# Latent rows, keys and values of the last token tile, made in the softmax attention's first group

## Chip, cores and metric

One core of a Trainium2 chip (trn2). The metric is the device time of one execution in microseconds (us); a kernel's time is the median of its runs.

## What is computed

One inference step of a decoder layer over a prompt of 1024 tokens (8 tiles of 128) and 8 single sample tokens. One input projection feeds two head groups: latent attention with softmax (8 heads) and gated linear attention, called GLA (4 heads). Their gated outputs go through one output projection and a layer norm. Cut to what matters here:

```python
q = (rms_norm(cq, q_norm_g) @ w_uq)             # queries, 8 heads of 64 + 32 (rotary)
ckv = rms_norm(ckv, kv_norm_g)                  # latent rows, 128 wide
kr = apply_rope(kr, cos, sin)                   # one rotary key for all heads
k_nope = einsum('bsr,rhn->bshn', ckv, w_uk)     # keys of the prompt
v      = einsum('bsr,rhv->bshv', ckv, w_uv)     # values of the prompt
# query block i (128 tokens) attends to keys of tiles 0..i
p = softmax(where(key_pos <= q_pos, s * MLA_SCALE, -inf)); o = p @ v
# GLA: chunkwise, with a state carried from tile to tile
state = exp(b_last) * state + (k * exp(b_last - b)).T @ v
```

## The kernel before

Every engine's instructions are written out by hand, in order, and engines meet through counting semaphores (`x.wait_ge(sem, n)` waits until a count is reached). T is 8, the number of token tiles. PSUM is addressed as `banks[:, 0..7, 512]`.

After the input projection come eight **slots**, `for k in range(T)`, one for each token tile of the GLA. On TensorE slot k runs, in this order: `latent_rows(k+1)` (L2014, four transposes of the next tile's latent query part, latent rows and rotary key into bank 6), `decays(k+1, 0)`, `forget_gate`, `near_products(k)` in three parts (L2090, 32 x 32 products) with `decays(k+1, 1)` between, `latent_keys(k+1)` (L2023, four products with `w_uk` into bank 6), the third part of `near_products(k)`, `far_products(k)`, the rest of the decays, `key_query_rows(k+2)`, `latent_values(k+1)` (L2029, one product with `w_uv` into bank 2), `gated_columns(k-1)` and `outputs(k)` (L2118, L2121, and L2126 for the state). `near_products(k)` waits for `S_ready` of tile k-1: VectorE (DVE) makes the new state at L1561 from the products of L2126. Slot 6 also holds the two `q_proj` of query block 0's tile (L2152), slot 7 their transposes (L2161) and the first scores (`head_scores(0)`, L2174).

The products of 32-bit operands run as two passes each, so one `nc.tensor.matmul` of them appears as two MATMUL records, each with a weight load (LDWEIGHTS, engine PEld).

ScalarE (ACT) brings the results out of PSUM: `latent_out` (L1068: L1073, L1074, L1075), `latent_keys_out` (L1077: L1080, twice) and `latent_values_out` (L1083: L1086). After each tile's rotary key is in place, SyncE (SP) spreads it to all heads by a DMA (L779).

Then come the 48 **steps** of the softmax attention, in four groups of 12. `GROUPS = ((6, 0), (4, 3), (5, 2), (7, 1))` names the query blocks of each group, and `TURNS[0] = "LLLLSLLSLLSS"` the order in the first group: L is one head of block 6, S two heads of block 0. Query block i reads keys and values of tiles 0 to i, so the last tile's keys and values are first read by block 7, in the fourth group (from step 36). Step s on TensorE: `head_scores(s)`; HEAD place; then at the TAIL place `weights_turned(s-2)` (L2383), `products(p)` of a finished pair of heads (L2302, before the table's pieces); then what the tables put there: `q_proj` and `q_transpose` of later query blocks through bank 7. ACT in step s: HEAD place; `transposed_out(s-2)` (L1253), `probabilities(s)` (L1244), TAIL place, where `q_half` (L1142) and `qt_half` (L1148) empty bank 7. DVE in step s: `mix` of a pair, the largest scores (L1710 and L1712), and the normalising of the step before (L1728).

Of the kernel before, what the change touches and what calls it, by code (L numbers as in the profile page):

```python
# [15 lines left out]
P = 128  # L16
# [88 lines left out]
def hybrid_step(nc, a, o):  # L105

    with ExitStack() as ctx:
# [483 lines left out]
        def q_bank(i, q):  # L591

            return 6 if i == 0 and q == 0 else 7

        def mixed_bank(t):

            return 1 if t < T - 2 else 6
# [19 lines left out]
                     (32, HEAD), (32, TAIL), (35, TAIL), (36, TAIL), (37, TAIL), (39, TAIL), (40, TAIL), (42, TAIL), (44, TAIL)]  # L617
        assert len(PIECES_AT) == PIECES and sorted(PIECES_AT) == PIECES_AT
        assert not set(PIECES_AT) & (set(PROJECTED_AT) | set(TURNED_AT))

        def piece_at(s, place):
            return PIECES_AT.index((s, place)) + 1 if (s, place) in PIECES_AT else 0
# [100 lines left out]
        def _(sp):  # L723
# [111 lines left out]
        def _(pool):  # L835
# [111 lines left out]
        def _(act):  # L947
# [120 lines left out]
            def latent_out(t):  # L1068
                act.wait_ge(a_transposed, t + 1)
                if t > 0:  # L1070
                    act.wait_ge(k_done, t)
                    act.wait_ge(kv_done, t)
                nc.scalar.activation(ckvT, banks[:, 6, QR:QR + P], ACT.Copy).then_inc(a_copied, 1)  # L1073
                nc.scalar.activation(z[:, t, 0:QR], banks[:, 6, 0:QR], ACT.Copy).then_inc(a_copied, 1)  # L1074
                nc.scalar.activation(KTh[NOPE:QK, 0, P * t:P * t + P], banks[NOPE:QK, 6, 384:512], ACT.Copy).then_inc(a_copied, 1)  # L1075

            def latent_keys_out(t):  # L1077
                act.wait_ge(k_done, t + 1)
                for q in range(2):
                    nc.scalar.activation(KTh[0:NOPE, q:H:2, P * t:P * t + P],  # L1080
                                         banks[NOPE * q:NOPE * q + NOPE, 6, :].rearrange("p (h s) -> p h s", h=4), ACT.Copy).then_inc(k_copied, 1)

            def latent_values_out(t):  # L1083
                act.wait_ge(kv_done, t + 1)
                act.wait_ge(kdec_ready, t + 1)
                nc.scalar.activation(z[:, t, W_GQ:W_GV], banks[:, 2, :], ACT.Copy).then_inc(v_copied, 1)  # L1086

            def key_query_out(t):
                act.wait_ge(qk_transposed, t + 1)
# [81 lines left out]
            for k in range(T):  # L1171
                if k == T - 1:
                    for q in range(2):
                        qt_half(0, q)
                if 0 <= k + 1 < T:
                    latent_out(k + 1)
                    decay(k + 1, 0)
                if k + 2 < T:
                    n_a = soft(k + 2)
                if 0 <= k + 1 < T:  # L1180
                    decay(k + 1, 1)
                    latent_keys_out(k + 1)
                if k >= 0:
                    far_blocks(k)
                if 0 <= k + 1 < T:
                    decay(k + 1, 2)
                    decay(k + 1, 3)
                    decay_rest(k + 1)
                if k + 2 < T:
                    key_query_out(k + 2)  # L1190
                if k == T - 2:
                    for q in range(2):
                        q_half(0, q)
                if 0 <= k + 1 < T:
                    latent_values_out(k + 1)
                if 0 <= k < T - 1:
                    n_a = o_stats(k)
# [88 lines left out]
            for s in range(len(STEPS) + LAG):  # L1286
                if s == 2:
                    act.wait_ge(gated_T, T)
                    act.wait_ge(S_out, 32)
                for place in (HEAD, TAIL):  # L1290
                    if place == TAIL:
                        if s == len(STEPS):
                            act.wait_ge(qt_done, 2 * T)
                        if s >= len(STEPS):
                            for j in range(2):
                                keys_out(0, 2 * (s - len(STEPS)) + j)
                        if s >= LAG:
# [590 lines left out]
        def _(pe):  # L1888
# [124 lines left out]

            def latent_rows(t):  # L2014
                pe.wait_ge(normed, 1)
                pe.wait_ge(qkT_copied, 2 * max(t, 1) + 2)
                if t == 1:
                    pe.wait_ge(k_copied, 2)
                for q in range(3):
                    nc.tensor.transpose(banks[:, 6, P * q:P * q + P], z[:, t, P * q:P * q + P], ident[:])  # L2020
                nc.tensor.transpose(banks[0:QK, 6, 384:512], z[:, t, W_KR - NOPE:W_GM], ident[:]).then_inc(a_transposed, 1)

            def latent_keys(t):  # L2023
                pe.wait_ge(a_copied, 3 * t + 3)
                for m in range(H // 2):
                    last = nc.tensor.matmul(banks[:, 6, P * m:P * m + P], w_uk[:, P * m:P * m + P], ckvT, start=True, stop=True)
                last.then_inc(k_done, 1)

            def latent_values(t):  # L2029
                if t > 0:  # L2030
                    pe.wait_ge(att_copied, 6 * t)
                nc.tensor.matmul(banks[:, 2, :], ckvT, w_uv[:], start=True, stop=True).then_inc(kv_done, 1)

            def gate_rows(t):
                if t > 0:
# [40 lines left out]
            def near_products(t, levels):  # L2076
                if levels[0] == 0:
                    pe.wait_ge(x_ready, t + 1)
                    pe.wait_ge(v_copied, t + 1)
# [169 lines left out]
            pe.wait_ge(padded, 6)  # L2249

            for k in range(T):
                if 0 <= k + 1 < T:
                    latent_rows(k + 1)
                    decays(k + 1, 0)
                if k + 2 < T:
                    forget_gate(k + 2)
# [6 lines left out]
                if 0 <= k + 1 < T:  # L2263
                    latent_keys(k + 1)
                if k == T - 1:
                    for q in range(2):
# [9 lines left out]
                    key_query_rows(k + 2)  # L2276
                if k == T - 2:
                    q_proj(0, 0)
                if 0 <= k + 1 < T:
                    latent_values(k + 1)  # L2280
                if k + 3 < T:
                    gate_rows(k + 3)
# [130 lines left out]
            for s in range(len(STEPS) + LAG):  # L2413
# [6 lines left out]
                for place in (HEAD, TAIL):  # L2420
                    if place == TAIL:
# [6 lines left out]
                        if s >= LAG:  # L2428
# [4 lines left out]
                            for p in range(N_PAIRS_OF_HEADS - 2):  # L2433
                                if last_step(p) == r - 1:
                                    products(p)
                    if (s, place) in PROJECTED_AT:
                        bank_of_queries((s, place))
                        q_proj(*PROJECTED_AT[s, place])
# [201 lines left out]
```

## Time and profile before

| | us |
|---|---|
| median of 3 runs | 745.68 |
| the runs | 745.23, 745.68, 751.47 |
| the profiled execution, its own time | 743.97 |
| span from its first to its last instruction | 742.1 |
| TensorE busy | 705.5 (95% of the span) |
| VectorE busy | 355.3 (48%) |
| ScalarE busy | 327.3 (44%) |
| GpSimd busy | 75.6 (10%) |

The mean granted TensorE clock is 0.995 of full speed. Slot 6 stands at 353.3 to 366.9 us of the span, slot 7 from there to 375.7, and steps 4 to 6 of the softmax attention at 388.7 to 399.7. The ends of matmuls are modelled, so two records that follow each other overlap in the listing; what a stretch of TensorE costs is read from the start of its first instruction to the start of the one behind it.

### The profile page before, as it was taken

The numbers are of one execution on the slowest core, as the hardware profiler recorded it, in microseconds if no ns is written. First come the engines' busy times: TensorE is split into PE (matmuls) and PEld (weight loads), VectorE is DVE, ScalarE is ACT, GpSimd is POOL, SyncE is SP. The second block draws the span as 40 slices with busy tenths as digits, with TensorE's granted clock in tenths as the row PEclk, the third lists the DMA queues.
The fourth block names the chain that finished last, engine by engine and source line by source line (L and its number), as shares of the span: only waits on it lengthen the run. The fifth ranks groups of instructions, "written<-read, shape, count | busy, mean of one in ns | idle before, by whom it ended". The sixth has DMA issues, their size and how long they took to land.

```text
span 742.1 us, 16684 instructions
## 1 busy us (share of the span) xinstructions
PE 705.5 (95%) x7025; PEld 546.4 (74%) x7025; DVE 355.3 (48%) x782; ACT 327.3 (44%) x779; POOL 75.6 (10%) x113
## 2 busy tenths in 40 slices
PE   2799999999999999999999999999999999999995
PEld 1486878788789986777766666777677889678884
DVE  0454380030202025777675576667671111389977
ACT  1254651121212137667656566645675667602100
POOL 0000000000000010101111201132113443000000
PEclk9999999999999999999999999999999999999999
DMA  9995300303001011000010000202756774103332
GB/s 293 396 375 174 114 0 1 114 0 97 0 1 57 1 43 51 9 14 11 10 11 1 1 1 1 59 1 76 240 183 222 274 267 175 60 1 116 123 132 85
DMA packets 35301, 70.31 MB, mean 95 GB/s; under 512 B 6626, under 2 KB 17979, under 8 KB 33564
## 3 DMA queue, kind: packets, MB, share of 16 engines
q1 hardware_dynamic: 30602, 47.73, 19.8%
q0 software_dynamic: 4016, 20.97, 8.1%
q8 instruction: 56, 0.92, 0.5%
q10 hardware_dynamic: 610, 0.55, 0.3%
q14 instruction: 17, 0.14, 0.1%
HBM read 62.26 MB, written 6.07 MB: 92 GB/s over the span
## 4 chain that ended last, share of the span: by engine, by line
PE 90%; DVE 3%; SPq 2%; DMA 2%; ACT 1%; issue 1%; another core or an unknown queue 1%; DVEq 0%; ACTq 0%
PE banks L1988 21%; PE banks L2174 8%; PE banks L2000 6%; PE banks L2302 5%; PE banks L2383 4%; PE banks L2403 3%; PE banks L2152 3%; PE banks L2512 3%; PE banks L2514 3%; PE banks L2513 2%; PE banks L2090 2%; PE banks L2009 2%; PE banks L2452 2%; PE banks L2471 2%; PE banks L2495 2%; DMA s_x<-in_x_prompt 2%
## 5 line engine op out<-in xcount | busy, mean ns | idle before, releaser
L1044 ACT ACTIVATE s_z<-banks 128x512 f32<-128x512 f32 (+3 forms) x40 | 19.6, 501 | 130.0 <-PE banks L1988 130.0
L1988 PE MATMUL banks<-s_w_parts,s_h_b 128*128 128x272 f32 (+3 forms) x328 | 68.0, 323 | 0.0
L1253 ACT ACTIVATE s_z<-banks 128x512 f32<-128x512 f32 (+2 forms) x88 | 41.4, 517 | 47.1 <-PE banks L2383 46.3
L1417 DVE COPY s_zs<-banks 8x512 f32<-8x512 f32 (+3 forms) x6 | 3.5, 576 | 118.5 <-PE banks L1962 118.5
L1988 PEld LDWEIGHTS banks<-s_w_parts,s_h_b 128*128 128x128 f32 x328 | 49.3, 189 | 4.9 <-issue 1.7
L1244 ACT ACTIVATE s_z<-banks,s_temps 128x896 f32<-128x896 f32 (+7 forms) x64 | 47.2, 742 | 11.6 <-DVE s_temps L1712 8.6
L1988 PE MATMUL banks<-s_w_parts,s_h_a 128*128 128x256 f32 (+2 forms) x256 | 49.7, 314 | 0.0
L1988 PE MATMUL banks<-s_z_r,s_h_b 128*128 128x512 f32 (+1 forms) x152 | 48.8, 387 | 0.0
L2383 PEld LDWEIGHTS banks<-s_ident,s_z 128*128 128x128 f32 x288 | 33.3, 141 | 11.8 <-issue 5.5
L2383 PE MATMUL banks<-s_ident,s_z 128*128 128x128 f32 x288 | 39.8, 274 | 1.6 <-DVE s_z L1728 1.6
L1988 PE MATMUL banks<-s_z_r,s_h_a 128*128 128x512 f32 x128 | 40.9, 395 | 0.0
L1988 PEld LDWEIGHTS banks<-s_w_parts,s_h_a 128*128 128x128 f32 x256 | 36.0, 189 | 3.6 <-issue 0.4
L2302 PE MATMUL banks<-s_z 128*64 128x128 f32 x576 | 38.5, 278 | 0.0
L1267 ACT ACTIVATE s_z<-banks 128x512 f32<-128x512 f32 x64 | 33.1, 602 | 9.3 <-PE banks L2403 7.6
L2302 PEld LDWEIGHTS banks<-s_z 128*64 128x64 f32 x576 | 30.8, 136 | 5.4 <-issue 5.4
L1350 ACT ACTIVATE s_temps<-s_temps,s_eps_t 128x1 f32<-128x1 f32 (+1 forms) x9 | 2.6, 294 | 72.2 <-DVE s_temps L1845 72.2
L1728 DVE TENSOR_SCALAR s_z<-s_z,s_temps 128x896 f32<-128x896 f32 (+7 forms) x64 | 33.2, 540 | 1.7
L1712 DVE TENSOR_REDUCE s_temps<-banks 128x1 f32<-128x896 f32 (+3 forms) x32 | 32.8, 1024 | 1.1
L1988 PEld LDWEIGHTS banks<-s_z_r,s_h_b 128*128 128x128 f32 x152 | 28.5, 188 | 5.6
L1988 PEld LDWEIGHTS banks<-s_z_r,s_h_a 128*128 128x128 f32 x128 | 24.0, 188 | 6.7 <-issue 0.8
L2174 PE MATMUL banks<-s_kt,s_temps 96*128 96x512 f32 (+1 forms) x64 | 25.9, 527 | 0.0
L2174 PE MATMUL banks<-s_kt,s_z 96*128 96x512 f32 (+2 forms) x64 | 25.2, 515 | 0.0
(391 smaller groups left out, 1520.7 us busy)
## 6 DMA issues: line engine op xcount, KB each, us to landing
s_z<-in_w_ada SPq DMA_DIRECT2D x16, 512.0 KB, 12.2
s_temps<-in_w_in SPq DMA_DIRECT2D x3, 2048.0 KB, 7.7
s_x<-in_x_prompt SPq DMA_DIRECT2D x8, 512.0 KB, 11.8
s_z<-in_w_ada SPq DMA_DIRECT2D x1, 4096.0 KB, 13.8
s_kt<-in_w_out SPq DMA_DIRECT2D x8, 512.0 KB
s_temps<-in_x_prompt SPq DMA_DIRECT2D x8, 512.0 KB
out_y_prompt<-s_temps SPq DMA_DIRECT2D x7, 512.0 KB
s_temps<-in_w_in SPq DMA_DIRECT2D x2, 832.0 KB, 14.2
```

The source lines that it names most:

```text
L1244: last = nc.scalar.activation(weights_of(s, u), score_of(s, u), ACT.Exp, bias=nmx[:, c:c + 1], accum_out=rsum[:, c:c + 1])
L1253: nc.scalar.activation(PTb[r % 3][:, 4 * g:4 * g + n, :], banks[:, 4 + (groups(r) + g) % 2, 0:P * n].rearrange("p (j q) -> p j q", j=n), A ...
L1267: nc.scalar.activation(latT(n, j), banks[:, j, :], ACT.Copy).then_inc(f_Tc, 1)
L1712: nc.vector.tensor_reduce(nmx[:, c:c + 1], score_of(s, 0), AX_X, ALU.max, negate=True).then_inc(mx_ready, 1)
L1728: last = nc.vector.tensor_scalar(weights_of(s, u), weights_of(s, u), rinv[:, c + u:c + u + 1], None, ALU.mult)
L1988: last = nc.tensor.matmul(banks[:, proj_bank(c, t), 0:WIDTH[c]], h_[half][:, k, n0:n0 + P], w_, start=(k == 0 and n == 0), stop=(k == KT - ...
L2000: last = nc.tensor.matmul(banks[:, proj_bank(1, u), :], w_[:, k, P * m:P * m + P], h_[half][:, k, :], start=(k == 0 and n == 0), stop=(k = ...
L2152: last = nc.tensor.matmul(banks[:, q_bank(n, q), 0:384], z[:, BLOCKS[n], P * k:P * k + P], w_uq[:, k, 384 * q:384 * q + 384], start=(k == ...
L2174: last = nc.tensor.matmul(score_of(s, u)[:, n0:n1], QTb[n % 4][:, h, :], KTh[:, h, n0:n1], start=True, stop=True)
L2302: last = nc.tensor.matmul(banks[64 * par:64 * par + 64, 6, 0:P], V(j, 2 * hp + par), block, start=(j == 0), stop=(j == i))
L2383: last = nc.tensor.transpose(banks[:, 4 + k0 % 2, P * (b % 4):P * (b % 4) + P], Pm[r % 3][:, P * b:P * b + P], ident[:])
L2403: last = nc.tensor.transpose(banks[:, j, P * r:P * r + P], cached(n, 4 * j + r), ident[:])
```

## The change

The three pieces of the last token tile (t = 7) leave slot 6 and go to three places of steps 4 and 5: the rows to (4, HEAD), the keys to (5, HEAD), the values to (5, TAIL), on TensorE and ScalarE alike. They use bank 7 in place of banks 6 and 2. The latent rows, transposed, go to the tile's own slab `z[:, 7, W_CKV:W_KR]` and not to `ckvT`, so ScalarE first waits for the output DMA that reads that slab (`kv_out`). The spreading DMA of the last tile moves behind SP's later transfers, GpSimd's wait becomes one tile shorter, and the scores of block 7 get the waits that were in slots 6 and 7.

```diff
+        def latent_bank(t):
+            return 6 if t < T - 1 else 7
+        def turned_latent(t):
+            return ckvT if t < T - 1 else z[:, T - 1, W_CKV:W_KR]
+        LAST_ROWS_AT, LAST_KEYS_AT, LAST_VALUES_AT = (4, HEAD), (5, HEAD), (5, TAIL)
...
 # SP
-            for t in range(T):
+            for t in range(T - 1):
+                rotary_keys_spread(t)
...
             sp.dma_start(o_new[:, :, 0:KVR], o["kv_sample"][:, :, 0, :].to_broadcast([H, NB, KVR])).then_inc(p_rows, 16)
+            rotary_keys_spread(T - 1)
...
 # POOL
-            pool.wait_ge(a_copied, 3 * T)
+            pool.wait_ge(a_copied, 3 * (T - 1))
...
 # ACT, latent_out(t)
+                if t == T - 1:
+                    act.wait_ge(kv_out, 32)
...
 # ACT, the slots
-                if 0 <= k + 1 < T:
-                    latent_out(k + 1)
+                if k + 1 < T - 1:
+                    latent_out(k + 1)
...
 # ACT, the steps
+                    if (s, place) == LAST_ROWS_AT:
+                        latent_out(T - 1)
+                    if (s, place) == LAST_KEYS_AT:
+                        latent_keys_out(T - 1)
+                    if (s, place) == LAST_VALUES_AT:
+                        latent_values_out(T - 1)
...
 # PE, latent_rows(t), latent_keys(t), latent_values(t)
+                if t == T - 1:
+                    pe.wait_ge(qp_copied, projected_before(LAST_ROWS_AT))
...
+                if t == T - 1:
+                    pe.wait_ge(qp_copied, projected_before(LAST_KEYS_AT))
...
+                if t == T - 1:
+                    pe.wait_ge(k_copied, 2 * T)
...
 # PE, q_proj(0, 0)
-                    pe.wait_ge(k_copied, 2 * T)
+                    pe.wait_ge(k_copied, 2 * (T - 1))
...
 # PE, head_scores(s)
+                if i == T - 1:
+                    pe.wait_ge(kr_in, 16 * T)
+                    pe.wait_ge(k_copied, 2 * T)
...
 # PE, slot 7
-                    pe.wait_ge(kr_in, 16 * T)
+                    pe.wait_ge(kr_in, 16 * (T - 1))
...
 # PE, bank_of_queries(at): before each q_proj and q_transpose of the steps
+                if at > LAST_ROWS_AT:
+                    pe.wait_ge(a_copied, 3 * T)
+                if at > LAST_VALUES_AT:
+                    pe.wait_ge(v_copied, T)
```

## Rows read from the trace of the kernel before

**Rows 1.** Stretch of steps 4, 5: span, busy time (count) of each engine, PEclk, DMA.
```profile
389.09:396.80 7.71, 7.71 (x56) 5.24 (x55) 3.61 (x10) 4.01 (x11) 2.33 (x4) 1.00 0.01 3
```
**Rows 2.** TensorE in order of time, slots 6, 7: start, us, instruction, idle before.
```profile
353.29 0.55 PE L2020 MATMUL banks<-s_ident,s_z 128*128 128x128 f32 x3
...
353.70 0.48 PE L2066 MATMUL banks<-s_act_parts,s_w_parts 128*128 128x512 f32 x1
...
354.34 0.35 PE L2090 MATMUL banks<-s_mixT 64*32 64x32 f32 x32
...
357.57 0.49 PE L2026 MATMUL banks<-s_temps,s_w_uk 128*128 128x128 f32 x3 [0.37 <-issue]
...
357.99 0.76 PE L2090 MATMUL banks<-s_temps 64*32 64x32 f32 x64
...
361.87 1.02 PE L2032 MATMUL banks<-s_w_uv,s_temps 128*128 128x512 f32 x2
362.73 0.60 PE L2139 MATMUL banks<-s_ident,s_temps 128*128 128x128 f32 x4
...
367.74 0.36 PE L2090 MATMUL banks<-s_mixT 64*32 64x32 f32 x32 [0.80 <-DVE s_temps L1561]
...
368.95 1.08 PE L2161 MATMUL banks<-s_ident,s_z 128*96 128x128 f32 x8
```
**Rows 3.** VectorE in order of time: the state of tiles 5, 6.
```profile
353.41 0.60 DVE L1561 SCALAR_TENSOR_TENSOR s_temps<-s_temps,banks 128x128 f32<-128x128 f32 x2 [0.19 <-PE banks L2126]
...
366.99 0.61 DVE L1561 SCALAR_TENSOR_TENSOR s_temps<-s_temps,banks 128x128 f32<-128x128 f32 x2 [2.33 <-PE banks L2126]
```
**Rows 4.** TensorE again: keys of slot 6 up to their pause, and of slot 5.
```profile
356.38 0.82 PE L2026 MATMUL banks<-s_temps,s_w_uk 128*128 128x128 f32 x5
...
345.15 1.16 PE L2026 MATMUL banks<-s_temps,s_w_uk 128*128 128x128 f32 x8
346.24 0.29 PE L2090 MATMUL banks<-s_temps 64*32 64x32 f32 x16
346.69 0.61 PE L2090 MATMUL banks<-s_temps 64*32 64x32 f32 x48 [0.16 <-issue]
```
**Rows 5.** The same view in slot 2, a longer pause.
```profile
311.66 0.25 PE L2107 MATMUL banks<-s_temps 64*32 64x32 f32 x4 [1.03 <-issue]
```
**Rows 6.** Counts between pauses (PE, then PEld, in brackets), and behind the last.
```profile
311.64:346.69 35.05, 34.77 (x757) 25.82 (x758) 26.59 (x80) 24.94 (x83) 2.25 (x4) 1.00 0.06 13
346.69:357.56 10.87, 10.51 (x253) 8.18 (x253) 8.04 (x25) 7.91 (x27) 1.41 (x3) 1.00 0.01 4
357.56:366.07 8.51, 8.50 (x126) 6.07 (x126) 5.67 (x17) 4.94 (x11) 0.84 (x2) 1.00 0.07 17
```
**Rows 7.** DMA queues at 309.3 to 309.4, 355.2 to 355.3 and 363.3 to 363.4.
```profile
q8 instruction: 1, 0.02, 57.6%
...
q8 instruction: 1, 0.02, 57.5%
...
q8 instruction: 1, 0.02, 60.0%
```
**Rows 8.** ScalarE in order of time, slot 6 and steps 3 to 5.
```profile
358.10 1.21 ACT L1080 ACTIVATE s_kt<-banks 64x512 f32<-64x512 f32 x2 [0.74 <-PE banks L2026]
...
388.87 0.50 ACT L1142 ACTIVATE s_z<-banks 128x384 f32<-128x384 f32 x1
...
395.23 0.98 ACT L1253 ACTIVATE s_z<-banks 128x512 f32<-128x512 f32 x2 [1.51 <-PE banks L2383]
...
396.19 1.01 ACT L1244 ACTIVATE s_z<-banks,s_temps 128x896 f32<-128x896 f32 x1
```
**Rows 9.** TensorE in order of time, steps 4 to 6.
```profile
389.09 0.93 PE L2383 MATMUL banks<-s_ident,s_z 128*128 128x128 f32 x7
...
394.53 0.93 PE L2383 MATMUL banks<-s_ident,s_z 128*128 128x128 f32 x7
395.30 1.67 PE L2174 MATMUL banks<-s_kt,s_z 96*128 96x512 f32 x4
```

More of the change, by code:

```diff
@@ L619, in hybrid_step @@
         assert not set(PIECES_AT) & (set(PROJECTED_AT) | set(TURNED_AT))
+        LAST_ROWS_AT, LAST_KEYS_AT, LAST_VALUES_AT = (4, HEAD), (5, HEAD), (5, TAIL)
+        assert not {LAST_ROWS_AT, LAST_KEYS_AT, LAST_VALUES_AT} & (set(PROJECTED_AT) | set(TURNED_AT) | set(PIECES_AT))
         def piece_at(s, place):
@@ L776, in _, with rotary_keys_spread @@
             sp.dma_start(w_uq[:], a["w_uq"].rearrange("(k p) n -> p k n", p=P)).then_inc(uq_in, 16)
-            for t in range(T):
+            def rotary_keys_spread(t):
                 sp.wait_ge(a_copied, 3 * t + 3)
@@ L1072, in latent_out @@
                     act.wait_ge(kv_done, t)
-                nc.scalar.activation(ckvT, banks[:, 6, QR:QR + P], ACT.Copy).then_inc(a_copied, 1)
-                nc.scalar.activation(z[:, t, 0:QR], banks[:, 6, 0:QR], ACT.Copy).then_inc(a_copied, 1)
-                nc.scalar.activation(KTh[NOPE:QK, 0, P * t:P * t + P], banks[NOPE:QK, 6, 384:512], ACT.Copy).then_inc(a_copied, 1)
+                if t == T - 1:
+                    act.wait_ge(kv_out, 32)
+                nc.scalar.activation(turned_latent(t), banks[:, latent_bank(t), QR:QR + P], ACT.Copy).then_inc(a_copied, 1)
+                nc.scalar.activation(z[:, t, 0:QR], banks[:, latent_bank(t), 0:QR], ACT.Copy).then_inc(a_copied, 1)
+                nc.scalar.activation(KTh[NOPE:QK, 0, P * t:P * t + P], banks[NOPE:QK, latent_bank(t), 384:512], ACT.Copy).then_inc(a_copied, 1)
             def latent_keys_out(t):
@@ L1080, in latent_keys_out @@
                     nc.scalar.activation(KTh[0:NOPE, q:H:2, P * t:P * t + P],
-                                         banks[NOPE * q:NOPE * q + NOPE, 6, :].rearrange("p (h s) -> p h s", h=4), ACT.Copy).then_inc(k_copied, 1)
+                                         banks[NOPE * q:NOPE * q + NOPE, latent_bank(t), :].rearrange("p (h s) -> p h s", h=4), ACT.Copy).then_inc(k_copied, 1)
             def latent_values_out(t):
@@ L1085, in latent_values_out @@
                 act.wait_ge(kdec_ready, t + 1)
-                nc.scalar.activation(z[:, t, W_GQ:W_GV], banks[:, 2, :], ACT.Copy).then_inc(v_copied, 1)
+                nc.scalar.activation(z[:, t, W_GQ:W_GV], banks[:, 2 if t < T - 1 else 7, :], ACT.Copy).then_inc(v_copied, 1)
             def key_query_out(t):
@@ L1181, in _ @@
                     decay(k + 1, 1)
+                if k + 1 < T - 1:
                     latent_keys_out(k + 1)
@@ L1193, in _ @@
                         q_half(0, q)
-                if 0 <= k + 1 < T:
+                if k + 1 < T - 1:
                     latent_values_out(k + 1)
@@ L2015, in latent_rows @@
                 pe.wait_ge(normed, 1)
-                pe.wait_ge(qkT_copied, 2 * max(t, 1) + 2)
+                pe.wait_ge(qkT_copied, min(2 * T, 2 * max(t, 1) + 2))
                 if t == 1:
                     pe.wait_ge(k_copied, 2)
+                if t == T - 1:
+                    pe.wait_ge(qp_copied, projected_before(LAST_ROWS_AT))
                 for q in range(3):
-                    nc.tensor.transpose(banks[:, 6, P * q:P * q + P], z[:, t, P * q:P * q + P], ident[:])
-                nc.tensor.transpose(banks[0:QK, 6, 384:512], z[:, t, W_KR - NOPE:W_GM], ident[:]).then_inc(a_transposed, 1)
+                    nc.tensor.transpose(banks[:, latent_bank(t), P * q:P * q + P], z[:, t, P * q:P * q + P], ident[:])
+                nc.tensor.transpose(banks[0:QK, latent_bank(t), 384:512], z[:, t, W_KR - NOPE:W_GM], ident[:]).then_inc(a_transposed, 1)
             def latent_keys(t):
                 pe.wait_ge(a_copied, 3 * t + 3)
+                if t == T - 1:
+                    pe.wait_ge(qp_copied, projected_before(LAST_KEYS_AT))
                 for m in range(H // 2):
-                    last = nc.tensor.matmul(banks[:, 6, P * m:P * m + P], w_uk[:, P * m:P * m + P], ckvT, start=True, stop=True)
+                    last = nc.tensor.matmul(banks[:, latent_bank(t), P * m:P * m + P], w_uk[:, P * m:P * m + P], turned_latent(t), start=True, stop=True)
                 last.then_inc(k_done, 1)
             def latent_values(t):
-                if t > 0:
+                if t == T - 1:
+                    pe.wait_ge(k_copied, 2 * T)
+                elif t > 0:
                     pe.wait_ge(att_copied, 6 * t)
-                nc.tensor.matmul(banks[:, 2, :], ckvT, w_uv[:], start=True, stop=True).then_inc(kv_done, 1)
+                nc.tensor.matmul(banks[:, 2 if t < T - 1 else 7, :], turned_latent(t), w_uv[:], start=True, stop=True).then_inc(kv_done, 1)
             def gate_rows(t):
@@ L2078, in near_products @@
                     pe.wait_ge(x_ready, t + 1)
-                    pe.wait_ge(v_copied, t + 1)
+                    pe.wait_ge(v_copied, min(t + 1, T - 1))
                     if t > 0:
@@ L2251, in _ @@
             for k in range(T):
+                if k + 1 < T - 1:
+                    latent_rows(k + 1)
                 if 0 <= k + 1 < T:
-                    latent_rows(k + 1)
                     decays(k + 1, 0)
@@ L2262, in _ @@
                     near_products(k, range(2, 4))
-                if 0 <= k + 1 < T:
+                if k + 1 < T - 1:
                     latent_keys(k + 1)
@@ L2278, in _ @@
                     q_proj(0, 0)
-                if 0 <= k + 1 < T:
+                if k + 1 < T - 1:
                     latent_values(k + 1)
@@ L2435, in _ @@
                                     products(p)
+                    if (s, place) == LAST_ROWS_AT:
+                        latent_rows(T - 1)
+                    if (s, place) == LAST_KEYS_AT:
+                        latent_keys(T - 1)
+                    if (s, place) == LAST_VALUES_AT:
+                        latent_values(T - 1)
                     if (s, place) in PROJECTED_AT:
```

## Prediction

> **What bounds the kernel now.** I read the busy times by stretch first, then TensorE in order of time through the two places that the change touches, then what ended its pauses. In steps 4 and 5 of the softmax attention TensorE is busy for 7.71 of 7.71 us, while DVE has 3.61 and ScalarE 4.01 [rows 1]. The listing of the slots shows instruction behind instruction, with few gaps [rows 2]. So TensorE's own order sets the time in both places: work taken out of a slot and put back in a step is no gain by itself. The gain or loss lies in the gaps that vanish or appear. Three kinds of gap are to be seen.
>
> One is a wait for another engine: in slot 7 `near_products(7)` starts at 367.74 after 0.80 us of idling [rows 2]. The state update on DVE starts at 366.99, lasts 0.61 and so ends at 367.60 [rows 3]; TensorE starts 0.14 later.
>
> The second kind has no releaser. In slot 6 the eight passes of `latent_keys(7)` break after the fifth [rows 4] and go on 0.37 us later [rows 2]; in slot 5 the same eight run without a break and the next part breaks instead [rows 4], in slot 2 `far_products` breaks for 1.03 us in mid-group [rows 5]. No semaphore stands there. Counting instructions between the breaks explains them: 757 + 758 = 1515 from the one at 311.66 to the one at 346.69, and 253 + 253 = 506 from there to 357.57 [rows 6]. That is 6 and 2 times 253, so a break stands where a block of instructions ends. A single packet of 0.02 MB on an instruction queue starts 2.3 us before two of these ends: at 309.3 for 311.66, at 355.2 for 357.57 [rows 7]. So TensorE's instructions come in blocks, each asked for about when the one before it is begun, and a block run through too fast must wait. `near_products` runs 64 matmuls in about 0.7 us (0.76 less the overlap [rows 2]), and a slot's are 192: fast enough.
>
> The Trainium skill, "Runtime: NRT & Kernel Launch", section "Instruction fetch mechanics", says that instructions are refilled in blocks of 256 and that crossing a block's end is mostly hidden. The trace agrees on the block (253 engine instructions, the rest would be bare waits) and not on "hidden": 0.37 and 1.03 us are exposed. By this rule of the Trainium skill the sum would be that of rival A below.
>
> The third kind is the turn of bank 7, emptied by ScalarE; it comes up where the pieces are put back.
>
> **What leaves slot 6.** `latent_rows(7)` takes 353.29 to 353.70, 0.41 us [rows 2]. Behind it stand `decays(7, 0)` and then `near_products(6)` at 354.34, which needs the state of tile 5: that is there at 353.41 + 0.60 = 354.01 [rows 3], plus the 0.14 seen above 354.15. So only 0.2 of the 0.41 can be gained. `latent_keys(7)` takes 356.38 to 357.99, 1.61 us with its break [rows 2, 4]. `latent_values(7)` takes 361.87 to 362.73, 0.86 us [rows 2]. By order alone the slot gives back 0.2 + 1.61 + 0.86 = 2.67 us. Nothing else comes to set it: DVE and ScalarE get their inputs earlier with TensorE, and ScalarE loses the copies L1073 to L1075, L1080 and L1086 of that tile.
>
> **What the blocks take back.** The end of the block moves with the instructions removed. Before the break there are 8 fewer (4 transposes with their loads) and one wait, and the 16 of the keys are cut too, so the end falls 10 matmuls into the third part of `near_products(6)`. The packet is asked for at the head of `near_products(6)`, just behind the wait for the state, which does not move. I therefore keep the time of release, 357.57, where TensorE would now arrive near 356.3. What is gained up to there is only the rest of the keys, 357.57 to 357.99, and 10 near products of 0.011 us: 0.42 + 0.11 = 0.53 us in place of 1.81. With the values, slot 6 gives 0.53 + 0.86 = **1.39 us**.
>
> The next block now ends in `outputs(6)`, at 366.07, 126 + 126 instructions behind the break [rows 6], and its successor was asked for early, at 363.3 [rows 7], since the queue reads ahead while long matmuls run. With 8 + 1 + 16 + 4 = 29 instructions gone, that end moves past the remaining `outputs(6)` and falls some 5 matmuls into `near_products(7)`, behind the wait for the state. The queue can't read past a wait that isn't met, so the next packet comes only after 367.7. From release in slot 6 I have the delay: state there at 354.01, block there at 357.57, 3.5 us. In slot 7: 367.60 + 3.55 = 371.15 in the old times. TensorE would reach that end four matmuls into the `q_transpose` that start at 368.95 [rows 2], at about 369.54. New pause: **1.6 us**. Lower bound nothing (the packet comes early, as at 363.3), upper 2.5 (estimate: the delay longer by 0.9, the spread of the breaks 0.16 to 1.03 [rows 4, 5]).
>
> **What comes in.** The rows 0.41, the keys without a break 345.15 to 346.24 = 1.09 [rows 4], the values 0.86: 2.36 us, all exposed, since TensorE has no gap there [rows 1]. Then three waits:
>
> - The rows now use bank 7 and wait for ScalarE's copy of `q_proj(2, 0)`. It ends at 388.87 + 0.50 = 389.37 [rows 8]; with 0.14 that is 389.51, and TensorE stands ready at 389.09 [rows 9]. Pause 0.4 us. Queued behind it: `weights_turned(2)`, `products(0)`, `q_proj(2, 1)`. Bounds 0.2 and 0.6.
> - The values use bank 7 behind the keys and wait for both key copies on ScalarE, 1.21 us, which began 0.1 after the last key product [rows 8]. Between them TensorE has only `weights_turned(3)`, 394.53 to 395.30 = 0.77 us [rows 9]. Pause 0.1 + 1.21 + 0.14 - 0.77 = 0.67 us. Queued behind: `head_scores(6)`. Bounds 0.4 and 0.9.
> - `q_transpose(2, 0)` waits for the value copy. ScalarE does before it the turned weights (0.98) and the probabilities of step 5 (1.01 and a read of 0.2) [rows 8], then 0.6; together 2.8 us behind the key copies, while TensorE has the pause's last 0.14, 0.86 of values and 1.50 of scores (its 1.67 less overlap [rows 9]). Pause about 0.1; bounds 0 and 0.5.
>
> Added: 2.36 + 0.4 + 0.67 + 0.1 = **3.53 us**.
>
> The rest costs nothing: SP's spreading DMA of tile 7 moves behind the `o_new` transfer, its data are wanted from step 36, and behind it in SP's queue stands the sample state, asked for only after a table piece of a later step. GpSimd's wait only gets shorter. `kv_out` was met when the slots began. If that cover failed, SP's queue would move by one DMA issue.
>
> **Sum.** -1.39 + 1.6 + 3.53 = +3.7 us on the profiled execution's 743.97, so 747.7. The median of the runs is 1.71 above that execution, which gives 745.68 + 3.7 = **749.4 us**.
>
> **Rivals.**
>
> A. Order alone: block ends cost no more than before, as if the reads ran ahead. -2.67 + 3.53 = +0.9 us, 746.5. For it: the packet at 363.3 came early. Against it: five-eighths of a key group followed by an idle 0.37. Chance 0.25. By the rule of the Trainium skill, "Runtime: NRT & Kernel Launch", section "Instruction fetch mechanics", it would come out here.
>
> B. Faster. The steps' TensorE stretch isn't really full: the ends of matmuls are modelled, and a listing of 100% would hide a wait for ScalarE's turned weights in each step. Then pieces and waits of 3.53 us hide under it and the 2.67 stays: 743.0. It decides for faster once less than 2.67 of the 3.53 is exposed and slot 7 has no pause. Against it: the starts follow each other at the same spacing as in other steps. Chance 0.10.
>
> C. Slower still: ScalarE's copies stand ahead of probabilities in its order; if the steps wait for their whole length, rows 0.9, keys 1.21 and values 0.6, 2.7 in place of 1.17, the sum is +5.2, 750.9. For it: ScalarE runs everything in order. Against: it is busy for half of these steps [rows 1]. Chance 0.15.
>
> My forecast has 0.50. A measurement of this kernel tells about 1% (7.5 us) from no change, and no case reaches that. Range 745.0 to 751.5: it leaves out B and the upper half of C. Chances: faster by over 1% 0.02, within 1% 0.95, slower by over 1% 0.03.
>
> **What would show it.** Right: in slot 6 a break inside the third part of `near_products`, ending near 357.6; `outputs(6)` 1.4 us earlier; in slot 7 a break of 1 to 2 us among the `q_transpose`; idling of 0.4 before the rows and 0.7 before the values; step 6 later than before by 3.7. Wrong: slot 7 without a break (A), steps 4 and 5 no longer than before (B), or a total outside the range.

## The result, and the profile after

The changed kernel takes 753.31 us (median of 20 executions, 747.58 to 757.01), beside 746.35 us for the kernel before (20 executions, 744.87 to 751.47). The ratio taken over the executions is 1.0073, 95% interval 1.0052 to 1.0094: +5.4 us, inside 1% as forecast. (The two medians alone differ by 6.96 us.) But the median lies above the range of 745.0 to 751.5. Of the miss of 3.9 us (753.31 against the forecast 749.4) the sum of the edits makes 0.5; the rest is in the step from one profiled execution to the median.

The profiled execution took 749.66 us (span 747.9, granted TensorE clock 0.995), 5.69 above that of before. Its first listing is TensorE in order of time in slots 6 and 7: start, us, instruction, idle before. L2119 is the old L2090 (near products), L2147 the old L2118, L2190 the old L2161.

```profile
355.70 0.36 PE L2119 MATMUL banks<-s_mixT 64*32 64x32 f32 x32
...
357.04 0.84 PE L2119 MATMUL banks<-s_temps 64*32 64x32 f32 x74
359.37 0.67 PE L2119 MATMUL banks<-s_temps 64*32 64x32 f32 x54 [1.49 <-issue]
...
368.21 0.36 PE L2119 MATMUL banks<-s_mixT 64*32 64x32 f32 x32 [0.80 <-DVE s_temps L1584]
...
369.42 0.75 PE L2190 MATMUL banks<-s_ident,s_z 128*96 128x128 f32 x5
371.84 0.49 PE L2190 MATMUL banks<-s_ident,s_z 128*96 128x128 f32 x3 [1.68 <-issue]
372.26 0.76 PE L2119 MATMUL banks<-s_temps 64*32 64x32 f32 x64
```

The state of tile 5, for which `near_products(6)` waits, in VectorE's order of time, and the count between the two pauses (span, then busy time with the count of PE and of PEld):

```profile
354.95 0.60 DVE L1584 SCALAR_TENSOR_TENSOR s_temps<-s_temps,banks 128x128 f32<-128x128 f32 x2 [0.24 <-PE banks L2155]
```
```profile
359.37:371.84 12.47, 9.99 (x253) 7.62 (x254) 7.99 (x24) 5.50 (x19) 2.44 (x4) 1.00 0.01 3
```

253 + 254 = 507 instructions lie between the pauses, two times 253 as between those of before [rows 6]. The keys' eight passes are gone from the middle; the pause that cut them [rows 2] now cuts the third part of `near_products(6)` after its tenth matmul (74 = 64 + 10), and a pause that was not there stands among the transposes of slot 7. One row of before, in the same view, fixes the end of that stretch:

```profile
369.96 0.76 PE L2090 MATMUL banks<-s_temps 64*32 64x32 f32 x64
```

Start differences, after less before, give the account. The state of tile 5, ahead of the first edit on TensorE, is there at 354.95 + 0.60 = 355.55 against 354.01 [rows 3]: this execution was 1.54 late before it reached the change. The head of `near_products(7)`: 368.21 - 367.74 = +0.47. So slot 6 gave 1.54 - 0.47 = 1.07. Behind the transposes: 372.26 - 369.96 = +2.30, so the new pause cost 1.83.

The lateness is older than the slots. The same VectorE copy in before and in after:

```profile
74.08 0.68 DVE L1417 COPY s_zs<-banks 8x512 f32<-8x512 f32 x1 [5.18 <-PE banks L1962]
```
```profile
76.28 0.68 DVE L1440 COPY s_zs<-banks 8x512 f32<-8x512 f32 x1 [6.24 <-PE banks L1985]
```

At 74 us of the span, far ahead of every edit, after was already 2.2 us late.

The instruction queue in the same execution, from 356.7 to 356.8 and from 369.2 to 369.3 us (packets, MB, share of 16 engines' time):

```profile
q8 instruction: 1, 0.02, 75.2%
...
q8 instruction: 1, 0.02, 82.6%
```

A share of a stretch of 0.1 us times 16 engines is the packet's time: 1.20 and 1.32 us, where [rows 7] gives 0.92. Both pauses end some 2.6 us after their packet begins (359.37, 371.84), before's 2.3. The packet of slot 7 begins 1.0 us behind the first instruction of `near_products(7)`; in the other traces that have this pause (again, left_out, ends_moved, spaced, again_long) it is 0.9 to 1.0 us too. In all six it begins behind the wait for the state, as forecast.

TensorE in steps 4 to 6, the same view, and the copies of ScalarE that bank 7 waits for:

```profile
390.95 0.61 PE L2206 MATMUL banks<-s_kt,s_qt 96*128 96x128 f32 x4
391.80 0.52 PE L2045 MATMUL banks<-s_ident,s_z 128*128 128x128 f32 x3 [0.24 <-ACT s_z L1157]
...
392.27 0.93 PE L2416 MATMUL banks<-s_ident,s_z 128*128 128x128 f32 x7
...
397.70 1.06 PE L2053 MATMUL banks<-s_z,s_w_uk 128*128 128x128 f32 x8
398.60 0.93 PE L2416 MATMUL banks<-s_ident,s_z 128*128 128x128 f32 x7
400.06 1.12 PE L2061 MATMUL banks<-s_w_uv,s_z 128*128 128x512 f32 x2 [0.53 <-ACT s_kt L1095]
401.02 1.67 PE L2206 MATMUL banks<-s_kt,s_z 96*128 96x512 f32 x4
402.58 0.61 PE L2190 MATMUL banks<-s_ident,s_z 128*96 128x128 f32 x4
```
```profile
391.17 0.49 ACT L1157 ACTIVATE s_z<-banks 128x384 f32<-128x384 f32 x1
...
398.80 1.21 ACT L1095 ACTIVATE s_kt<-banks 64x512 f32<-64x512 f32 x2 [1.91 <-PE banks L2053]
```

Against [rows 9]: 392.27 - 389.09 = +3.18, 398.60 - 394.53 = +4.07, 401.02 - 395.30 = +5.72. From +2.30 at the end of slot 7 the rows add 0.88, the keys 0.89 and the values with their wait 1.65: 3.42 in all. Behind that the difference stays at 5.7 to 5.8 to the end. What the change made of this execution is 5.72 - 1.54 = **+4.2 us**, forecast +3.7.

### The profile page after: what moved, and what is told of

It is laid out like the page before. It is cut to its first block, busy times and chain, and to the rows that moved or that the text cites. A ratio compares the mean times of both kernels' runs of the same rounds, so it can differ in the third digit from the quotient of the medians.

```text
span 747.9 us, 16716 instructions
## 1 busy us (share of the span) xinstructions
PE 706.4 (94%) x7025; PEld 545.9 (73%) x7025; DVE 355.1 (47%) x782; ACT 327.5 (44%) x779; POOL 75.4 (10%) x113
## 4 chain that ended last, share of the span: by engine, by line
PE 89%; DVE 3%; DMA 2%; ACT 2%; issue 2%; another core or an unknown queue 1%; ACTq 1%; DVEq 0%
PE banks L2011 20%; PE banks L2206 8%; PE banks L2023 6%; PE banks L2335 5%; PE banks L2416 4%; PE banks L2440 3%; PE banks L2181 3%; PE banks L2555 2%; PE banks L2557 2%; PE banks L2556 2%; PE banks L2119 2%; PE banks L2032 2%; PE banks L2495 2%; PE banks L2514 2%; PE banks L2538 2%
```

## The experiments

There were eleven runs in three comparisons, each on another chip and with its own executions of before; what each kernel does is told behind the two tables. Executions of one kernel differ in the mean clock granted to TensorE (0.979 to 0.996), and their times follow it. So beside the ratio stands a level at equal clock: a straight line fitted through all executions of a comparison, one slope for all kernels and one level for each (standard error behind it). The slopes are 592, 635 and 551 us for a whole unit of clock, which is 5.5 to 6.3 us for 0.01. The level puts the clock aside whatever lowered it, so a loss of clock that a kernel causes itself is not in it.

| kernel | ratio to before, 95% | executions, mean clock | us over before at equal clock |
|---|---|---|---|
| again | 1.0068 [1.0043, 1.0093] | 6, 0.9877 | +3.1 (0.5) |
| ends_back | 1.0049 [1.0031, 1.0068] | 7, 0.9884 | +2.3 (0.4) |
| left_out | 1.0011 [0.998, 1.0042] | 12, 0.9899 | +0.3 (0.3) |
| twice | 1.004 [1.0019, 1.006] | 12, 0.9918 | +3.3 (0.3) |
| ends_moved | 0.9987 [0.9962, 1.0011] | 12, 0.9919 | +0.9 (0.3) |
| spaced | 1.0033 [1.0012, 1.0054] | 12, 0.9923 | +3.6 (0.3) |
| spaced_back | 1.0034 [1.001, 1.0059] | 12, 0.9898 | +2.4 (0.3) |
| left_out_back | 0.9979 [0.9959, 0.9999] | 12, 0.9907 | -1.6 (0.3) |
| before_alone | 1.0009 [0.9992, 1.0025] | 12, 0.9903 | 0 (its executions count as before's) |
| again_long | 1.0077 [1.0043, 1.0111] | 7, 0.9900 | +4.0 (0.4) |
| ends_back_long | 1.007 [1.0047, 1.0092] | 6, 0.9883 | +3.0 (0.5) |

Before itself has a mean clock of 0.9910 (24 executions), 0.9899 (35) and 0.9922 (18) in the three. Its median there is 742.75, 747.16 and 742.17 us, so a time is compared only with its own before. The profiled executions show where they part: from 551 to 612 us of the span, far behind the change, the seven of the first and third comparison gain 3.7 to 4.2 us on the first trace of before, whatever the kernel, while the four of the second and after stay within 0.2 of it. Why is open.

Each profiled execution can also be read by itself, which leaves out what came before the slots and behind the steps. The marks are VectorE's state of tile 5 (353.41 in before), of tile 6 (366.99), of tile 7 (375.81) and a copy at 409.03. Us more than in before between them (* has a stretch at half clock in it):

| trace | slot 6 | slot 7 | steps |
|---|---|---|---|
| after | -1.07 | +1.83 | +3.48 |
| again | -1.33 | +3.08* | +3.49 |
| again_long | -1.03 | +1.56 | +3.49 |
| spaced | -1.33 | +3.82* | +3.49 |
| ends_back | -1.21 | 0.00 | +3.49 |
| ends_back_long | -0.76 | 0.00 | +3.49 |
| spaced_back | -1.21 | 0.00 | +3.48 |
| left_out | +0.50* | +3.37* | 0.00 |
| left_out_back | -1.30 | 0.00 | 0.00 |
| twice | -0.08 | 0.00 | +3.49 |
| ends_moved | -0.40 | +1.56 | 0.00 |
| before_alone | +0.28 | 0.00 | 0.00 |

So the steps cost the same 3.5 us wherever the pieces stand in them, and the price in slot 7 comes and goes with the block ends alone. The two traces of the changed kernel without a fall of the clock there give +4.2 and +4.0 us in all.

**again**: the changed kernel, unchanged.

> The changed kernel itself, again, beside the kernel before on the same chip. Its one profiled execution was at a mean granted clock of 0.995 and took 749.66 us, but the median of its 20 runs is 753.31, and most of those runs had a clock of 0.983 to 0.993. Theory 1 (order and instruction blocks make +4 us, the rest is TensorE's clock, granted at half speed in more stretches because TensorE now pauses longer around slots 6 and 7): ratio 1.007 to 1.009; an execution with a clock below 0.995 shows stretches at half clock near slot 6 or 7 or steps 2 to 6. Theory 2 (the clock has nothing to do with the change, the 20 runs fell on slower chips): ratio 1.005 or less, and half-clock stretches, if any, stand somewhere else.

Ratio 1.0068, just under Theory 1's 1.007 and well over Theory 2's 1.005: the loss of the first result comes back. Its trace also holds two stretches among the slots and steps in which TensorE was granted half its clock, one of them at a place that Theory 1 named. The view is busy time by stretch (count), then PEclk:

```profile
370.63:374.04 3.41, 3.41 (x96) 2.80 (x96) 1.73 (x6) 1.45 (x4) 0.00 (x0) 0.50 0.02 5
490.10:496.90 6.80, 6.80 (x53) 5.14 (x50) 2.96 (x9) 2.04 (x7) 0.97 (x1) 0.50 0.00 0
```

The first stands right behind the new pause. TensorE in order of time there:

```profile
366.87 0.36 PE L2119 MATMUL banks<-s_mixT 64*32 64x32 f32 x32 [0.80 <-DVE s_temps L1584]
...
370.54 0.74 PE L2190 MATMUL banks<-s_ident,s_z 128*96 128x128 f32 x3 [1.71 <-issue]
...
373.93 1.73 PE L2206 MATMUL banks<-s_kt,s_z 96*128 96x512 f32 x4
```

From the head of `near_products(7)` to the scores this takes 7.06 us; in the first trace, with a pause as long and no fall of the clock, 368.21 to 374.08, 5.87. So 3.4 us at 1.2 GHz in place of 2.4 cost 1.2 us. One fall behind one pause fits Theory 1's claim, that the pauses bring the falls; it does not show it.

**ends_back**: the changed kernel, with seven near products of slot 6 issued twice. That adds 28 instructions (7 products, 2 passes each, with their loads), about as many as left the slots (29), so that the blocks behind them end about where they did.

```diff
+  for again in range(2 if t == T - 2 and n == 0 and (hp, g, par) < (0, 3, 1) else 1):
       last = nc.tensor.matmul(banks[...], left, right, start=True, stop=True)
```

> The changed kernel with 7 of the first near products of slot 6 issued twice (28 engine instructions, the same result): every instruction block of TensorE behind them ends 28 instructions earlier in the work, about where it ended before the change, in slot 7 ahead of the wait for the state. If the breaks of 1.49 us in slot 6 and 1.68 us in slot 7 are block ends: the break among the q_transpose of slot 7 is gone (-1.7 us), the one of slot 6 moves to the last products of the second part and ends at the same time (+0.15), in sum -1.5 us on an execution at the same clock, ratio to before 1.004 or less, and less if fewer pauses also mean a better clock (Theory 1 above). Rival: the breaks come from work or waits of the slots; then nothing moves and the ratio stays at 1.007.

```profile
359.23 0.79 PE L2120 MATMUL banks<-s_temps 64*32 64x32 f32 x68 [1.22 <-issue]
...
368.16 0.36 PE L2120 MATMUL banks<-s_mixT 64*32 64x32 f32 x32 [0.80 <-DVE s_temps L1584]
...
369.37 1.08 PE L2191 MATMUL banks<-s_ident,s_z 128*96 128x128 f32 x8
370.37 0.76 PE L2120 MATMUL banks<-s_temps 64*32 64x32 f32 x64
```

The eight transposes of slot 7 run through. From the head of `near_products(7)` to its third part it is 2.21 us, as before (369.96 - 367.74 = 2.22), and 4.05 with the pause: the pause of slot 7 is a block's end and nothing else. The ratio of 1.0049 misses the expected 1.004 or less. The mean clock rose little (0.9884 for 0.9877), where Theory 1 hoped for more.

**ends_moved** puts the same question to the old order: the kernel before with seven near products of slot 5 left out (so 28 instructions fewer, its output is not whole) and no piece moved.

```diff
+  if t == T - 3 and n == 0 and (hp, g, par) < (0, 3, 1):
+      continue
```

> The kernel before, all in its old places, with 7 near products of slot 5 left out (28 engine instructions; those scores of the linear attention keep stale values). Nothing moves but the ends of TensorE's instruction blocks, 28 instructions later in the work, as the change does it. If block ends alone make the break of slot 7: a break of 1.5 to 1.9 us among the q_transpose of slot 7, and the break of 0.37 us in the keys of slot 6 gone or later in the third part of the near products; in sum +1.2 us at the same clock, and a mean granted clock lower than that of before (the first group had 0.991 for before and 0.988 for the changed kernel), ratio 1.002 to 1.004. Rival (the break needs the moved pieces): no break in slot 7, ratio 0.9995.

```profile
358.35 1.16 PE L2026 MATMUL banks<-s_temps,s_w_uk 128*128 128x128 f32 x8
...
370.52 0.75 PE L2163 MATMUL banks<-s_ident,s_z 128*96 128x128 f32 x5
372.63 0.53 PE L2163 MATMUL banks<-s_ident,s_z 128*96 128x128 f32 x3 [1.36 <-issue]
```

With all pieces where they were, the keys of slot 6 run unbroken and the transposes of slot 7 break behind the same fifth one. Taking instructions away made the kernel no quicker: the ratio is 0.9987 (interval 0.9962 to 1.0011), and it is 0.9 us slower at equal clock. The ratio of 1.002 to 1.004 that was expected did not come, and the mean clock, expected below before's, was 0.9919 for 0.9899: a pause of 1.36 us and no lower clock.

**left_out**: the changed kernel without the three pieces at all (the last tile's keys are zeros, its latent rows and values are not made), which leaves the slots' half of the sum. It leaves out the spreading DMA of that tile as well.

> The changed kernel without the three pieces at all: rows, keys and values of the last tile are left out (its keys are zeros), so slots 6 and 7 are those of the changed kernel and the steps those of the kernel before. It measures the slots' half alone. Instruction blocks: slot 6 gives 1.1, slot 7 loses 1.8, +0.7 us, ratio 1.001. By order alone (the blocks cost nothing): -2.7 us, ratio 0.9965. If the breaks are what lowers the clock, the clock is below that of before here too and the ratio is up to 1.005.

```profile
360.11 0.68 PE L2113 MATMUL banks<-s_temps 64*32 64x32 f32 x54 [1.44 <-issue]
...
374.12 0.49 PE L2184 MATMUL banks<-s_ident,s_z 128*96 128x128 f32 x3 [1.59 <-issue]
```

The forecast's slot half is -1.39 + 1.6 = +0.2 us; measured +0.3 (0.3) at equal clock. So work worth 2.67 us by order alone left the slots, and no gain came of it. In this trace both pauses were followed by 3.4 us at half clock, which begin 1.9 and 1.6 us behind their ends:

```profile
362.02:365.42 3.40, 3.40 (x9) 2.12 (x8) 3.30 (x10) 1.76 (x5) 0.00 (x0) 0.50 0.00 0
375.68:379.08 3.40, 3.40 (x23) 2.12 (x24) 2.21 (x6) 0.92 (x3) 0.00 (x0) 0.50 0.00 0
```

With slot 6's +0.50 in place of about -1.1 and slot 7's +3.37 in place of about 1.7, the falls cost some 1.6 us each here.

**twice**: the kernel before, its slots as they were, and the three pieces made a second time in steps 4 and 5, which is the other half.

> The kernel before with the three pieces made in slot 6 as before and a second time in steps 4 and 5, at the changed kernel's places (the second turn leaves the last tile's query rows unturned, so the last block's output is another). It measures the steps' half alone: 2.4 us of products and 1.0 to 1.2 us of waits for ScalarE, +3.4 to 3.5 us, ratio 1.0046. Rival (TensorE's time in the steps is not full, so the pieces hide): less than 2.7 us, ratio below 1.0036. If the waits of the steps are what lowers the clock: ratio up to 1.008.

TensorE in order of time, steps 4 to 6:

```profile
389.59 0.93 PE L2420 MATMUL banks<-s_ident,s_z 128*128 128x128 f32 x7
...
395.92 0.93 PE L2420 MATMUL banks<-s_ident,s_z 128*128 128x128 f32 x7
...
398.34 1.67 PE L2210 MATMUL banks<-s_kt,s_z 96*128 96x512 f32 x4
```

Against [rows 9] the difference grows from +0.50 over +1.39 to +3.04: 0.89 for the keys, 1.65 for the values with their wait, the same to 0.01 us as in the changed kernel. At equal clock the steps' half costs +3.3 (0.3), forecast 3.53. The two halves add up to 3.6, beside 3.1 and 4.0 for the changed kernel.

**left_out_back**: left_out with the seven products issued twice, so without pieces and with the old block ends.

> The three pieces left out (the last tile's keys are zeros) and 7 near products of slot 6 issued twice. Left out alone was 1.0011 with a break of about 1.5 us in slot 7. If that break is a block end, it is gone: 1.5 us less, ratio 0.999, and the clock at least that of before. It is the slots' half at its best: by order alone it would be 0.9965.

At -1.6 (0.3) us against left_out's +0.3, it is the only kernel whose ratio lies below 1 with its whole interval (0.9979), and it leaves work out. Of the order gain that the forecast put at 2.67 us, 1.6 shows once the ends are back (1.3 in the trace); with the moved ends nothing is left of it. The rest is not accounted for in full: the pause of slot 6 is still there (1.12 us).

**spaced**: the changed kernel with the pieces further from other users of bank 7.

```diff
-  2: ((3, TAIL), (4, TAIL), (6, HEAD), (6, TAIL)), 3: ((7, TAIL), (8, TAIL), (10, HEAD), (11, HEAD))
+  2: ((3, TAIL), (4, TAIL), (6, TAIL), (7, TAIL)), 3: ((8, HEAD), (8, TAIL), (10, HEAD), (11, HEAD))
-  LAST_ROWS_AT, LAST_KEYS_AT, LAST_VALUES_AT = (4, HEAD), (5, HEAD), (5, TAIL)
+  LAST_ROWS_AT, LAST_KEYS_AT, LAST_VALUES_AT = (5, HEAD), (5, TAIL), (6, HEAD)
```

> The changed kernel with the pieces one place later each, rows at (5, HEAD), keys at (5, TAIL), values at (6, HEAD), and the query turns behind them moved on, so that each copy of ScalarE has scores, turned weights or products over it. The same products in the same slots and group. If the three waits in the steps are worth the 1.1 us that the trace shows: 1.0 us less than the changed kernel at the same clock, ratio to before about 1.005 in place of 1.0068, and if the pauses of the steps also lower the clock, 1.004. Rival (the waits cover something else that then shows): ratio as the changed kernel's, 1.0065 or more.

```profile
370.80 0.49 PE L2190 MATMUL banks<-s_ident,s_z 128*96 128x128 f32 x3 [1.98 <-issue]
...
399.01 1.16 PE L2053 MATMUL banks<-s_z,s_w_uk 128*128 128x128 f32 x8 [0.17 <-ACT s_kt L1090]
...
402.09 1.13 PE L2061 MATMUL banks<-s_w_uv,s_z 128*128 128x512 f32 x2 [0.41 <-ACT s_kt L1095]
```

The 1.0 us that was expected did not come. The waits did not go, they moved: 0.17 + 0.41 = 0.58 us in place of 0.24 + 0.53 = 0.77. Its steps cost 3.49 us, exactly as in the changed kernel, and at equal clock it stands at +3.6, no better than the changed kernel. Its ratio of 1.0033 looks like a gain because its executions had the highest mean clock of all, though its trace has the longest pause (1.98) and half clock behind it.

**spaced_back**: both mends together.

> Both mends: the pieces spaced and 7 near products of slot 6 issued twice, so that the block ends lie as before the change. Slots: +0.7 - 1.5 = -0.8 us against before, steps: 2.4 us of products and about 0.1 of waits, in sum +1.7 us at the same clock, ratio 1.0025. If the changed kernel's lower clock comes from its pauses (1.49 and 1.68 us in the slots, 1.1 in the steps), the mean clock is that of before, 0.991. If the clock stays at 0.988, the pauses of the steps and the break of slot 7 are not its cause, and the ratio is 1.005.

1.0034; at equal clock +2.4 (0.3), 1.2 below spaced. Four kernels with the old ends against the four without them: -0.8, -1.0, -1.2, -1.9 us. The pause is worth about 1.2 us in the runs, where the traces without a fall have 1.56 to 1.83 in slot 7; the runs do not show where the difference lies. The steps' waits were expected to shrink to about 0.1 and the whole to +1.7, which failed as in spaced. Neither of the two placings of the pieces in the steps beat before.

**before_alone, again_long, ends_back_long**: before, the changed kernel and ends_back once more, to settle whether the lower clock belongs to the change and to its pause.

> The kernel before, unchanged, beside itself: it gives the size of what the comparison itself makes. Ratio to before 1.000 within 0.002; mean granted TensorE clock of its executions within 0.002 of that of the other executions of before.

> The changed kernel once more, unchanged, in more executions. Theory (instruction blocks and waits cost 4.2 us as its profiled execution shows, and the pauses bring more stretches in which TensorE is granted half its clock): ratio 1.0065 to 1.008, mean granted clock 0.002 to 0.003 below that of before on this chip. Rival (the clock varies from execution to execution whatever the kernel, and the earlier means of 0.9877 and 0.9890 were chance): ratio 1.0045 to 1.006, mean clock within 0.001 of before's.

> The changed kernel with seven near products of slot 6 issued twice, once more, in more executions: no pause in slot 7. Theory (stretches at half clock stand behind the pause in slot 7): mean clock above that of again_long by 0.001 or more, ratio 1.004 to 1.005. Rival (the clock has nothing to do with that pause): mean clock within 0.001 of again_long's, ratio lower than again_long's by the pause alone less the 0.3 us that the repeated products and the pause in slot 6 cost, 0.0015 to 0.002.

The trace of before_alone, which is the kernel before, has a stretch at half clock too:

```profile
483.12:493.35 10.23, 10.23 (x63) 7.37 (x62) 4.72 (x13) 3.75 (x10) 1.95 (x2) 0.50 0.00 0
```

TensorE in order of time there, and then in the first trace of before, where the clock stayed up:

```profile
482.89 1.37 PE L2383 MATMUL banks<-s_ident,s_z 128*128 128x128 f32 x6
...
487.47 2.92 PE L2174 MATMUL banks<-s_kt,s_z 96*128 96x512 f32 x4
...
493.70 1.46 PE L2174 MATMUL banks<-s_kt,s_z 96*128 96x512 f32 x4
```
```profile
483.19 0.87 PE L2383 MATMUL banks<-s_ident,s_z 128*128 128x128 f32 x6
...
485.90 1.56 PE L2174 MATMUL banks<-s_kt,s_z 96*128 96x512 f32 x4
...
489.24 1.46 PE L2174 MATMUL banks<-s_kt,s_z 96*128 96x512 f32 x4
```

10.81 us against 6.05: 4.8 us lost, and the execution's mean clock is 0.988 in place of 0.995. That stretch lies around products of 8 columns and of 1 column for the sample tokens (16 of 8 columns start at 481.01, those of 1 column at 485.68), far behind every edit. It fell there in again, ends_back, ends_moved, ends_back_long and before_alone, with and without the change, and not in the other traces. again_long has both pauses, 1.53 and 1.40 us, and no fall in the slots, the steps or behind them until the last 5 us of the kernel:

```profile
357.49 0.67 PE L2119 MATMUL banks<-s_temps 64*32 64x32 f32 x54 [1.53 <-issue]
...
369.68 0.49 PE L2190 MATMUL banks<-s_ident,s_z 128*96 128x128 f32 x3 [1.40 <-issue]
```

Its ratio of 1.0077 and its mean clock, 0.0022 below before's, are what the theory had. But ends_back_long, without the pause of slot 7, has a mean clock of 0.9883 and 1.007 where the theory wanted a higher clock and 1.004 to 1.005, and its trace has a fall right behind a pause in slot 1 that every kernel has, before too:

```profile
296.99:300.40 3.41, 3.41 (x94) 3.06 (x90) 0.73 (x3) 2.21 (x5) 1.12 (x2) 0.50 0.13 28
```

So the theory that the lower clock belongs to the pause of slot 7 falls. Its rival, a clock within 0.001 of again_long's, did not come true either (0.0017 lower). before_alone (0.9903) and the other executions of before beside it (0.9922) differ by 0.0019 with the same code, so means over a dozen executions can't carry a difference of that size.

## Why the prediction was right and wrong

**Slot 6**, forecast -1.39: -1.07. The pause stands exactly where it was counted to, ten matmuls into the third part. Its end was taken to stay where it was, 357.57 - 354.01 = 3.56 us behind the state of tile 5; it came 359.37 - 355.55 = 3.82 behind it. That is 0.26 more, and the packet took 0.28 longer (1.20 for 0.92).

**The block ends' price in slot 7**, forecast 1.6 (0 to 2.5): 1.83. Right in place, behind the fifth transpose where I had the fourth, and in cause: ends_back takes it away and ends_moved makes it in the old order. The delay from state to block was put at 3.55 us; here the state was there at 367.45 + 0.60 = 368.05 and the block at 371.84, 3.79. The row of the state in the trace after:

```profile
367.45 0.60 DVE L1584 SCALAR_TENSOR_TENSOR s_temps<-s_temps,banks 128x128 f32<-128x128 f32 x2 [1.51 <-PE banks L2155]
```

Rival A is out in every trace with the pieces gone from the slots and the ends not put back: slot 7 has a pause of 1.40 to 1.98 us in each. The Trainium skill, "Runtime: NRT & Kernel Launch", section "Instruction fetch mechanics", says that crossing a block's end is mostly hidden. The trace of after disagrees for this stretch: 1.49 and 1.68 us are exposed.

**The steps**, forecast 2.36 + 0.4 + 0.67 + 0.1 = 3.53: 3.42 in the trace, 3.3 in twice. The wait before the rows is 0.24 in the listing (0.4 by start differences: the rows' 0.88 less 0.47 of transposes), that before the values 0.53 for 0.67, the keys 0.89 for 1.09, and the third wait, forecast at 0.1, did not show. The forecast's own terms for it give more, 2.79 us on ScalarE against 0.14 + 0.86 + 1.50 = 2.50 on TensorE, so 0.3 and not 0.1; the miss is small either way. Rivals B (hidden) and C (whole copies) are out.

**The failed step** is the last one: "The median of the runs is 1.71 above that execution, which gives 745.68 + 3.7 = 749.4 us". It took before's profiled execution for the start and the distance from there to the median of three runs for a constant, and has no term for the clock at all. Two things that vary from execution to execution stood in its place. One is where an execution stands ahead of the change: after's profiled one was 2.2 us late at 74 us and 1.54 late at the state of tile 5 (there the other traces stood from 0.6 early to 2.3 late, kernels in the old order among both, so it is not the change). The other is mostly the clock: after's profiled execution had 0.995, its 20 executions 0.9890 in the mean, and their median lies 3.65 above it, not 1.71; by the slopes 0.006 of clock is 3.3 to 3.8 us. Before's own distance, over 20 executions, is 2.38. The miss is 0.48 (the sum, 4.18 for 3.7) + 1.54 (the start) + 1.94 (3.65 - 1.71) = 3.96, against 753.31 - 749.4 = 3.91. That the 1.54 fell on this execution is chance; whether the 1.94 is, stays open below. The range failed for the same reason: it was made from the bounds of the edits alone, though the three runs of before already reached from 745.23 to 751.47.

**What stays open** is whether the change lowers the clock. By the ratios the loss is 5.0 to 5.7 us, at equal clock 3.1 and 4.0, so 1.7 to 2.0 us of it is clock. At 0.992 or more were 43 of 89 executions of before and 8 of 33 of the changed kernel; of ends_back 2 of 13; of the other six kernels 38 of 72, among them spaced, which has all pieces in the steps and the longer pause. Part of the mean clock is set far from the change: near 25 us of the span every trace has a stretch at half clock, 3.4 us long in seven and 6.8 in six. I have no mechanism that fits all of these. Falls behind the pauses of slots 6 and 7 are seen in three traces (again, left_out, spaced) and not in after, again_long and ends_moved, which have the pause of slot 7 as well. What was shown is that such a fall costs 1.2 to 1.7 us there, and up to 4.8 at the sample products.

## What to carry to other kernels

A piece taken out of an instruction stream moves every later block end by its count of instructions: count where the next ends fall, and add the delay from the last unmet wait to the block if one falls just behind it. Work moved between two stretches that TensorE fills is worth the difference of its gaps, here no gain on one side and two new waits on the other. A forecast made on one profiled execution needs the spread between executions in its range; compare the granted clocks before taking an offset over.

## What the runs showed of the hardware

- A block of about 253 matmuls and weight loads that is run through quickly behind a wait leaves TensorE idle at its end: 1.1 to 2.0 us in slots 6 and 7 of the kernels with fewer instructions ahead or with products repeated (0.3 to 0.6 in slot 6 of before and twice). TensorE goes on 2.3 to 2.9 us after the packet begins; the packet's own time there was 0.92 to 1.47 us. Fewer instructions can be no quicker (ends_moved).
- TensorE's granted clock falls to 1.2 GHz in some executions of a program and not in others: behind pauses of 0.9 to 2.0 us, and around products of 8 columns and 1 column though TensorE is listed as busy there (10.23 of 10.23 us). One stretch costs 1.2 to 4.8 us, where the whole change costs 4.2 in the trace.
